# Cached value rows of the samples' attention: pairs in five slots, two of them idle slots of the weight ring

## The chip, the cores and the metric

The kernel runs on one core of one Trainium2 chip. The metric is the device time of one execution in microseconds (us), median of several runs. TensorE is PE, VectorE is DVE, ScalarE is ACT, GpSimd is POOL; SP issues most of the weight DMAs.

## The reference, cut to what matters

The reference is one inference step of a two-layer decoder: a Mamba-2 mixer, then a dilated windowed attention, each followed by a mixture of experts. It runs for one prompt of 256 tokens and for 8 samples of one new token each. The change touches only the samples' attention over their caches, in the second layer:

```
for g, (window, dil) in enumerate(((128, 1), (512, 4), (2048, 16))):
    q, k, v = qkv[:, :, g, 0], qkv[:, :, g, 1], qkv[:, :, g, 2]
    buf = kv_bufs[g]                                  # 8 samples, min(window, 1024) rows, k and v, 16 heads x 64
    k_all = concatenate([buf[:, :, 0], k]); v_all = concatenate([buf[:, :, 1], v])
    idx = wl - dil * arange(window // dil + 1)        # every dil-th row: 128, 128 or 64 of the cache, and the own row
    s = einsum('bshd,bskhd->bshk', q, k_all[:, idx]) * ATTN_SCALE
    p = exp(s - max(s)); l = sum(p)
    outs.append(einsum('bshk,bskhd->bshd', p, v_all[:, idx]) / l)
```

So each sample and each of the three head groups needs 128, 128 or 64 cached value rows of 1024 float32 numbers (512 or 256 KB), 24 such tiles in all. The groups are then combined by their softmax denominators.

## The kernel before, in words

**Engines and order.** Each engine has its own program, written out by hand, and semaphores tie them together. The weights go through a ring of six slots of 2 MB (`ring`), filled by SP in the order of use: ten plus four chunks of the first layer, the 32 experts of layer 0, then 20 chunks of the attention (`ATT_CHUNKS`: 18 of the q, k, v projection and two of the output projection), then the 32 experts of layer 1. A chunk may land when the products that read its slot's last chunk are done.

**The attention.** For each head group g, PE projects 24 column tiles (`qkv_tile`, 16 products of 264 columns each): eight of q, eight of k, eight of v. With the eight v tiles go eight steps t of the prompt's attention: `scores`, the tile, then `lagging(g, t)`, which turns the probabilities of step t - 1 (`turn`, L1200) and multiplies the values of step t - 2 (`values`, L1212). DVE masks and takes maxima (`masked`), divides in the last group (`divided`), and takes the products up (`taken_up`). ACT does the exponents and copies.

**The samples' caches.** POOL loads key rows and queries (`keys`, `query`) into `rows_in`, a tile of `CSLOTS` = 5 slots of 1024 numbers per partition: three slots of keys, two of queries. DVE multiplies and sums them (`cache_scores`; semaphore `k_r`). When all 20 jobs are done, POOL loads the value rows with `cached_values(n)` (L702 to L706) for n = 0 to 23, one tile into slot n % 5 of the same `rows_in`. From the sixth load on it waits for `v_p`, which PE raises once per tile used.

In the last head group, at steps 3 to 6, PE runs `cache_values(i)` (L1266 to L1283), i = 0 to 3, for samples 2i and 2i + 1. It takes the groups in turn; for each it waits for both samples' tiles (`r_l`) and issues eight products at L1279 (the helper splits each float32 product in two). That is six tiles and 24 products for one i: 16 with 128 keys and 8 with 64. The sum for i stands in one bank. DVE masks it (`own_rows(i)`, L2233) one step later, behind `masked` and ahead of `taken_up`, and PE gathers the channels (`own_channels(i)`, L1285, products at L1294) ahead of the next `cache_values`. POOL's stores of the new value rows stand behind all 24 loads in its program.

**The ring's idle slots.** Chunk 14 and chunk 15 of the attention (k tiles 56 to 63 of the last group) lie in slots 4 and 5. In `moe_stream(1)` (L439) SP refills slots 4 and 5 first, on `moes[1].gu` >= 1, then slots 0 and 1 on >= 2, then slots 2 and 3 on the output projection's tiles 3 and 7. Tile 63 raises `moes[1].gu` first and tile 71, the last projected, raises it second; all other tiles raise `q_p`.

Of the kernel before, what the change touches and what calls it, by code (L numbers as in the profile page):

```python
# [12 lines left out]
D = 1024  # L13
DT = D // P
TP = 256
NS = 8
# [28 lines left out]
NGRP = len(PATTERNS)  # L45
KEYS = [min(w, PAST) // dil for w, dil in PATTERNS]
SCALE = HD ** -0.5
NEG = -1.0e30
CSLOTS = 5
KSLOTS = 3  # L50
JOBS = 1 + 2 * DT
CJOBS = [(g, b, 1) for g in range(2) for b in range(NS)] + [(2, b, 2) for b in range(0, NS, 2)]

# [15 lines left out]
RING = 6  # L69
SSM_CHUNKS = (IN_DIM - SH) // 512 + DI * D // (P * CH)  # L70
ATT_CHUNKS = NGRP * 3 * D // 512 + D * D // (P * CH)
STREAM_SLOT = (0, (SSM_CHUNKS + 3 * NE) % RING)
# [3 lines left out]
def bass_hybrid_step(nc, a, outs):  # L76
# [6 lines left out]
    with ExitStack() as ctx:  # L83
# [9 lines left out]
        ring = sb("ring", [P, RING, CH])  # L93
# [55 lines left out]
        m = Area()  # L149
# [40 lines left out]
        m = Area(after_vec)  # L190
        st_in = m(STATES, NS, N)
        outer = m(2, NS, N)
        m = Area(0)
# [4 lines left out]
        m = Area()  # L198
# [25 lines left out]
        m = Area(after_vec + STATES * NS * N)  # L224
# [5 lines left out]
        m = Area(ARENA - DT * (EG + NE))  # L230
# [3 lines left out]
        m = Area()  # L234
# [8 lines left out]
        rows_in = m(CSLOTS, D)  # L243
# [127 lines left out]
        moes = [Moe(0), Moe(1)]  # L371
# [3 lines left out]
        q_p = sem("qkv_projected")  # L375
# [12 lines left out]
        r_l = [sem(f"cache_rows_landed{i}") for i in range(CSLOTS)]  # L388
# [5 lines left out]
        v_p = sem("cache_values_summed")  # L394
# [25 lines left out]
        def cache_rows(g, b, kv):  # L420

            w, dil = PATTERNS[g]
            return caches[g][0, b, :, kv].rearrange("(n s) h d -> s n (h d)", s=dil)[0]

        def wait_chunk(eng, n):

            eng.wait_ge(s_ld[n % RING], 16 * (n // RING + 1))
# [112 lines left out]
        def _(pool):  # L540
# [84 lines left out]
            for t in range(XT_TILES):  # L625
                g = t // TPG
# [53 lines left out]
            def keys(u):  # L680
                g, b, n = CJOBS[u]
                if u >= KSLOTS:
                    pool.wait_ge(k_r, u - KSLOTS + 1)
                for i in range(n):
                    pool.dma_start(rows_in[i * HD:i * HD + KEYS[g], u % KSLOTS, :],
                                   cache_rows(g, b + i, 0)).then_inc(r_l[u % KSLOTS], 16)

            def query(u):
                g, b, n = CJOBS[u]
                slot = KSLOTS + u % 2  # L690
                if u >= 2:
# [7 lines left out]
                    keys(u)  # L699
                    query(u)  # L700

            def cached_values(n):  # L702
                b, g = 2 * (n // 6) + n % 2, n % 6 // 2
                if n >= CSLOTS:
                    pool.wait_ge(v_p, n - CSLOTS + 1)
                pool.dma_start(rows_in[0:KEYS[g], n % CSLOTS, :], cache_rows(g, b, 1)).then_inc(r_l[n % CSLOTS], 16)  # L706

            for g in range(NGRP):
                if g >= 1:
                    cache_jobs(range(NS * (g - 1), NS * g))  # L710
                pool.wait_ge(kv_e, JOBS * g + 1)
                pool.dma_start(q_rows[g].rearrange("b (t d) -> t b d", d=P),
                               q_own).then_inc(q_st, 16)
                if g == NGRP - 1:
                    pool.wait_ge(q_st, 16 * NGRP)
                    cache_jobs(range(2 * NS, len(CJOBS)))
                else:
                    pool.wait_ge(q_st, 16 * (g + 1))
                lo = 1 if g == 0 else 0
                rows = kv_p[g][0, 0].rearrange("(c p) w h d -> p c w (h d)", p=P)  # L720
                own_rows = kv_s[g][0].rearrange("b s w h d -> (s w) b (h d)").rearrange("w b (t d) -> w t b d", d=P)
                for kind in range(2):
                    if g == NGRP - 1 and kind == 1:
                        pool.wait_ge(k_r, len(CJOBS))
                        for n in range(NS * NGRP):
                            cached_values(n)
                    for q in range(2):
                        pool.wait_ge(kv_e, JOBS * g + 1 + DT * kind + 4 * q + 4)
                        pool.dma_start(rows[:, :, kind, 512 * q:512 * q + 512],
                                       KV[:, lo:2, 512 * q:512 * q + 512]).then_inc(kvst, 16)  # L730
                    pool.dma_start(own_rows[kind], kv_own).then_inc(kvst, 16)
# [5 lines left out]
        def _(pe):  # L737
            def transpose(out, in_):
                return pe.transpose(out, in_, ident[0:in_.shape[0], 0:in_.shape[0]])  # L739
# [323 lines left out]
            for i in range(CT):  # L1063
# [5 lines left out]
                for k in range(DT):  # L1069
                    if i == 0:  # L1070
                        tile_ready(0, k)
                    mm = pe.matmul(bank[i % 2][:, 0:T], wv[:, k, (i % 4) * P:(i % 4 + 1) * P], hT[:, k, :],  # L1072
                                   start=(k == 0), stop=(k == DT - 1))
# [23 lines left out]
            for t in range(XT_TILES):  # L1097
                g = t // TPG
# [24 lines left out]
            for d in range(DT):  # L1123
                if d < 2:
                    mm = out_products(d, LAST, XT_TILES)
                else:
# [3 lines left out]
                    mm = out_products(d, 0, XT_TILES)  # L1130
# [14 lines left out]
            def qkv_tile(i):  # L1145

                n = i // 4
                slot = (STREAM_SLOT[1] + n) % RING
                if i % 4 == 0:
                    pe.wait_ge(loads[1][slot], 16 * (n // RING + 1))  # L1150
                if i >= 2:
                    pe.wait_ge(q_e, i - 1)
                wv = ring[:, slot, :].rearrange("p (k n) -> p k n", k=DT)
                for k in range(DT):
                    if i == 0:
                        tile_ready(2, k)
                    mm = pe.matmul(bank[i % 2][:, 0:T], wv[:, k, (i % 4) * P:(i % 4 + 1) * P], hT[:, k, :],  # L1157
                                   start=(k == 0), stop=(k == DT - 1))

                mm.then_inc(moes[1].gu if i in (63, 71) else q_p, 1)  # L1160
                if i == 0:
                    pe.matmul(bank[7][:, 0:P], half[:, :], half[:, :], start=True, stop=True).then_inc(c_p, 1)

            def rows_job(g, j):

                n = JOBS * g + j
                if n:
# [32 lines left out]
            def turn(g, t, h):  # L1200
                n = DT * g + t
                if g < 2:
                    pe.wait_ge(h_e, 4 * (n + 1))
                else:
                    pe.wait_ge(h_n, t + 1)
                if n or h:
                    pe.wait_ge(h_c, 2 * n + h)
                for j in range(3):
                    mm = transpose(bank[4][:, j * P:(j + 1) * P], sm[:, t % 2, h, j * P:(j + 1) * P])
                mm.then_inc(h_t, 1)  # L1210

            def values(g, t):  # L1212
# [50 lines left out]
            before = [sum(j[2] for u, j in enumerate(CJOBS) if u % KSLOTS == slot) for slot in range(KSLOTS)]  # L1263
            before += [sum(j[2] for u, j in enumerate(CJOBS) if u % 2 == slot) for slot in range(2)]

            def cache_values(i):  # L1266
                if i == 0:
                    pe.wait_ge(c_a, 2 * NGRP + 3)
                    pe.wait_ge(c_v, 11)
                else:  # L1270
                    pe.wait_ge(y_o, i)
                for g in range(NGRP):
                    n0, k = 6 * i + 2 * g, KEYS[g]
                    for n in (n0, n0 + 1):
                        pe.wait_ge(r_l[n % CSLOTS], 16 * (before[n % CSLOTS] + n // CSLOTS + 1))
                    for q in range(2):
                        for j in range(2):
                            r = 64 * j + 32 * q
                            mm = pe.matmul(bank[5][r:r + 2 * DT, :], pTs[0:k, g, 2 * i + j:P:NS],  # L1279
                                           rows_in[0:k, (n0 + j) % CSLOTS, 512 * q:512 * q + 512],  # L1280
                                           start=(g == 0), stop=(g == NGRP - 1))
                            if q:
                                mm.then_inc(v_p, 1)  # L1283

            def own_channels(i):  # L1285

# [53 lines left out]
            for d in range(DT):  # L1340
                n = ATT_CHUNKS - 2 + d // 4
                slot = (STREAM_SLOT[1] + n) % RING
# [4 lines left out]
                for k in range(DT):  # L1347
                    if d == 0:
                        pe.wait_ge(h_o, 2 * DT + k + 1)
                    mm = pe.matmul(bank[d % 2][:, 0:T], wv[:, k, (d % 4) * P:(d % 4 + 1) * P], yT[:, k, :],  # L1350
                                   start=(k == 0), stop=(k == DT - 1))
# [10 lines left out]
        def _(act):  # L1362
# [170 lines left out]
            for i in range(CT + 2):  # L1533
                if i < CT:
# [4 lines left out]
                    b = bank[i % 2]  # L1539
# [5 lines left out]
                if i >= 2:  # L1545
                    j = i - 2
# [40 lines left out]
            norm(2, xn_a, gmix(1))  # L1587

            def qkv_done(i):
                if i in (63, 71):  # L1590
                    act.wait_ge(moes[1].gu, 1 if i == 63 else 2)
                else:
                    act.wait_ge(q_p, i + 1 - (i > 63))

            def copy_tile(g, i):

# [110 lines left out]
        def _(v):  # L1707
# [392 lines left out]
            for t in range(XT_TILES + 1):  # L2100
                g = t // TPG
# [129 lines left out]
                v.memset(bank[5][:, :], 0.0).then_inc(c_v, 1)  # L2231

            def own_rows(i):  # L2233
                v.wait_ge(v_p, 6 * i + 6)
                if i >= 1:
                    v.wait_ge(c_p, 4 + i)
                v.tensor_tensor(y_own, bank[5][:, :], own_head, ALU.mult).then_inc(y_o, 1)
                v.wait_ge(c_p, 5 + i)
                v.tensor_copy(y_c[:, 16 * i:16 * i + 16], bank[2][:, 16 * i:16 * i + 16]).then_inc(y_cp, 1)
# [73 lines left out]
```

## Time and profile before

| | us |
|---|---|
| median of 3 runs | 1778.4 |
| lowest, highest | 1776.05, 1779.36 |
| the profiled execution | 1779.78 |
| its span | 1778.1 |
| PE busy | 1667.8 (94%) |
| DVE busy | 642.9 (36%) |
| ACT busy | 451.2 (25%) |
| POOL busy | 132.9 (7%) |
| DMA, mean of the span | 302 GB/s |

Busy shares are averages over stages with different limits. The profile's rows give for each group of instructions how long the engine was busy and how long it stood idle just before, with the name of what ended that wait. "PEclk" is the TensorE clock that was granted, as a share of full speed.

### The profile page before, as it was taken

What the parts mean: (1) busy time and instruction counts of PE and PEld (TensorE: products, weight loads), DVE (VectorE), ACT (ScalarE), POOL (GpSimd) and SP (SyncE); (2) the same over time, 40 slices, a digit from 0 to 9 for tenths busy, and PEclk for the clock granted to TensorE, in tenths of its full rate; (3) what the DMA queues carried; (4) which work ended last, traced back from release to release, by engine and by line L of the source; (5) the groups of instructions that cost most, each with busy time, mean ns of one, the idle gap of its engine ahead of it and who ended that gap; (6) DMA issues with size and microseconds to landing.
All of it is one profiled execution on the core that took longest, in us unless ns stands there. A gap on an engine that the chain in (4) does not pass through costs nothing.

```text
span 1778.1 us, 21545 instructions
## 1 busy us (share of the span) xinstructions
PE 1667.8 (94%) x8029; PEld 971.2 (55%) x8029; DVE 642.9 (36%) x1382; ACT 451.2 (25%) x1166; POOL 132.9 (7%) x280
## 2 busy tenths in 40 slices
PE   7999879899999999999999999887899999999997
PEld 5887666734443344434877778655654443444342
DVE  2558992322222222214034354633432221222123
ACT  3439861211111111112142241222211111111112
POOL 1122430000000000001001002211000000000000
PEclk9999989899999999998999999988999999999999
DMA  9457772389999999999436619935259999999995
GB/s 324 144 169 209 205 241 105 100 339 417 429 429 428 429 428 429 429 428 347 149 108 221 237 64 336 271 118 185 95 227 417 430 429 427 430 429 427 429 428 211
DMA packets 101362, 537.72 MB, mean 302 GB/s; under 512 B 7964, under 2 KB 32740, under 8 KB 76690
## 3 DMA queue, kind: packets, MB, share of 16 engines
q1 hardware_dynamic: 85520, 485.18, 67.3%
q0 software_dynamic: 15360, 51.30, 9.0%
q8 instruction: 40, 0.66, 0.1%
q10 hardware_dynamic: 418, 0.39, 0.1%
q14 instruction: 24, 0.20, 0.0%
HBM read 520.61 MB, written 16.42 MB: 302 GB/s over the span
## 4 chain that ended last, share of the span: by engine, by line
PE 65%; DMA 17%; DVE 11%; ACT 3%; issue 2%; POOL 0%; SPq 0%; ACTq 0%; DVEq 0%
PE bank L834 20%; DMA ring<-in_moe_w_gate_up 13%; PE bank L1157 9%; PE bank L846 8%; PE bank L820 6%; PE bank L1072 5%; PE bank L739 4%; PE bank L1115 3%; PE bank L840 3%; DMA arena<-sample_queries 2%; PE bank L1350 2%; DVE arena L2072 2%; ACT arena L1654 1%; PE bank L1195 1%; DVE arena L2080 1%
## 5 line engine op out<-in xcount | busy, mean ns | idle before, releaser
L834 PE MATMUL bank<-ring,arena 128*64 128x512 f32 x2048 | 448.1, 593 | 20.6 <-DMA ring<-in_moe_w_gate_up 19.4
L834 PEld LDWEIGHTS bank<-ring,arena 128*64 128x64 f32 x2048 | 153.9, 137 | 308.2 <-issue 308.2
L1157 PE MATMUL bank<-hT,ring 128*128 128x264 f32 x1152 | 274.2, 395 | 0.0
L1157 PEld LDWEIGHTS bank<-hT,ring 128*128 128x128 f32 x1152 | 218.8, 194 | 46.0 <-issue 10.1
L846 PE MATMUL bank<-ring,arena 128*64 128x512 f32 x1024 | 226.8, 595 | 0.0
L1933 DVE TENSOR_TENSOR arena<-arena,bank 128x512 f32<-128x512 f32 x32 | 34.3, 1071 | 412.8 <-ACT arena L1436 412.8
L846 PEld LDWEIGHTS bank<-ring,arena 128*64 128x64 f32 x1024 | 70.6, 137 | 134.9 <-issue 134.9
L840 PE MATMUL bank<-arena 128*128 128x512 f32 x272 | 134.9, 618 | 1.7 <-ACT arena L1446 1.6
L739 PE MATMUL bank<-ident,arena 128*128 128x128 f32 (+6 forms) x609 | 104.9, 286 | 30.0 <-DMA arena<-in_ssm_d 10.4
L739 PEld LDWEIGHTS bank<-ident,arena 128*128 128x128 f32 (+6 forms) x609 | 73.6, 146 | 92.6 <-issue 46.5
L1436 ACT ACTIVATE arena<-bank 128x512 f32<-128x512 f32 x32 | 19.1, 597 | 412.7 <-PE bank L834 412.7
L1881 DVE SCALAR_TENSOR_TENSOR arena<-arena 128x1024 f32<-128x1024 f32 x34 | 43.7, 1284 | 211.4 <-ACT arena L1446 211.2
L820 PE MATMUL bank<-arena 128*128 128x224 f32 x512 | 103.8, 363 | 0.0
L1876 DVE TENSOR_TENSOR X<-X,bank 128x512 f32<-128x512 f32 x136 | 90.2, 683 | 26.8 <-PE bank L840 26.8
L820 PEld LDWEIGHTS bank<-arena 128*128 128x128 f32 x512 | 99.1, 197 | 0.8
L1072 PE MATMUL bank<-hT,ring 128*128 128x264 f32 x384 | 92.1, 401 | 0.0
L840 PEld LDWEIGHTS bank<-arena 128*128 128x128 f32 x272 | 45.9, 188 | 69.4 <-issue 51.4
L1072 PEld LDWEIGHTS bank<-hT,ring 128*128 128x128 f32 x384 | 75.1, 198 | 13.7 <-issue 0.4
L1613 ACT ACTIVATE arena<-bank 128x264 f32<-128x264 f32 x72 | 27.6, 384 | 156.5 <-PE bank L1157 156.5
L1444 ACT ACTIVATE arena<-bank 128x512 f32<-128x512 f32 x32 | 19.1, 597 | 189.5 <-PE bank L846 189.5
L1115 PE MATMUL bank<-arena,ring 128*128 128x264 f32 x256 | 62.5, 404 | 0.0
L1866 DVE TENSOR_TENSOR arena<-bank,vcol 128x448 f32<-128x448 f32 x64 | 40.0, 624 | 59.3 <-PE bank L820 59.3
(322 smaller groups left out, 1550.2 us busy)
## 6 DMA issues: line engine op xcount, KB each, us to landing
ring<-in_moe_w_gate_up SPq DMA_DIRECT2D x128, 2048.0 KB, 16.3
ring<-in_moe_w_down SPq DMA_DIRECT2D x64, 2048.0 KB, 12.9
ring<-in_attn_qkv SPq DMA_DIRECT2D x18, 2048.0 KB, 8.9
ring<-in_ssm_in_proj SPq DMA_DIRECT2D x10, 2048.0 KB, 15.3
arena<-in_cache_kv_w POOLq DMA_DIRECT2D x32, 512.0 KB, 6.9
out<-arena POOLq DMA_DIRECT2D x24, 512.0 KB, 3.9
ring<-in_ssm_out_proj SPq DMA_DIRECT2D x4, 2048.0 KB, 10.2
arena<-in_state_ssm SPq DMA_DIRECT2D x16, 512.0 KB, 4.8
```

Of the source, the lines that this page charges most:

```text
L739: return pe.transpose(out, in_, ident[0:in_.shape[0], 0:in_.shape[0]])
L820: mm = pe.matmul(bank[4 + i % 2][:, c * 4 * FREE:(c + 1) * 4 * FREE], xn_e[:, t, d * P:(d + 1) * P], Pm[:, t, :, :].rearrange("p e s -> p ...
L834: mm = pe.matmul(bank[j][e * SLOTS:(e + 1) * SLOTS, :], Xg[:, 4 * half + k, 2 * h + e, :], weights(2 * half + e)[:, k, j * DE:(j + 1) * DE ...
L840: pe.matmul(bank[6 + j % 2][:, :], CmT[:, (j // 2) * P:(j // 2 + 1) * P], ysl[:, j % 2, :], start=True, stop=True).then_inc(s.sc, 1)
L846: mm = pe.matmul(bank[2 + q][e * SLOTS:(e + 1) * SLOTS, :], actT[:, k, e * SLOTS:(e + 1) * SLOTS], weights(4 + e)[:, k, q * 512:(q + 1) * ...
L1072: mm = pe.matmul(bank[i % 2][:, 0:T], wv[:, k, (i % 4) * P:(i % 4 + 1) * P], hT[:, k, :], start=(k == 0), stop=(k == DT - 1))
L1115: mm = pe.matmul(bank[d % 2][:, 0:T], wv[:, k, (d % 2) * P:(d % 2 + 1) * P], conv_out[:, k, :], start=(k == 0), stop=(k == XT_TILES - 1))
L1157: mm = pe.matmul(bank[i % 2][:, 0:T], wv[:, k, (i % 4) * P:(i % 4 + 1) * P], hT[:, k, :], start=(k == 0), stop=(k == DT - 1))
L1350: mm = pe.matmul(bank[d % 2][:, 0:T], wv[:, k, (d % 4) * P:(d % 4 + 1) * P], yT[:, k, :], start=(k == 0), stop=(k == DT - 1))
L1866: v.tensor_tensor(Xg[:, 2 * i:2 * i + 2, :, NS:SLOTS], bank[4 + i % 2][:, 0:8 * FREE].rearrange("p (d e s) -> p d e s", d=2, e=4), gffn_fo ...
L1876: v.tensor_tensor(xs, xs, bank[6 + j % 2][:, :], ALU.add).then_inc(done, 1)
L1881: v.scalar_tensor_tensor(out=acc_s[:, :, :], in0=ysl[:, :, :], scalar=wcol[:, bass.ds(n, 1)], in1=acc_s[:, :, :], op0=ALU.mult, op1=ALU.ad ...
```

## The change

The value rows land in pairs, one pair for both samples of a step and one group, in five pair slots (`VSLOTS`). Pair slots 0 to 3 are halves of ring slots 4 and 5, and pair slot 4 is the first two slots of `rows_in`. Each pair is still loaded with two DMAs. Up to ten loads are out at once. `v_p` is raised once per pair, and a load of pair m from 5 on waits for `v_p` >= m - 4. Ahead of the first load POOL waits for all 64 tiles up to tile 63 (`q_p` >= 64), after which nobody reads the ring's slots 4 and 5. Tile 63 therefore raises `q_p` like the others; tile 71 raises `moes[1].gu` first, and the first transpose of the last prompt step raises it second. So SP refills ring slots 4 and 5 after tile 71 and slots 0 and 1 after that transpose.

```diff
+VSLOTS = 5
+        def value_rows(m):
+            if m % VSLOTS == VSLOTS - 1:
+                return rows_in[:, 0:2, :]
+            slot = (STREAM_SLOT[1] + ATT_CHUNKS - 6 + m % VSLOTS // 2) % RING
+            at = m % VSLOTS % 2 * 2 * D
+            return ring[:, slot, at:at + 2 * D].rearrange("p (j d) -> p j d", j=2)
...
-            def cached_values(n):
-                b, g = 2 * (n // 6) + n % 2, n % 6 // 2
-                if n >= CSLOTS:
-                    pool.wait_ge(v_p, n - CSLOTS + 1)
-                pool.dma_start(rows_in[0:KEYS[g], n % CSLOTS, :], cache_rows(g, b, 1)).then_inc(r_l[n % CSLOTS], 16)
+            def cached_values(m):
+                i, g = m // NGRP, m % NGRP
+                if m >= VSLOTS:
+                    pool.wait_ge(v_p, m - VSLOTS + 1)
+                for j in range(2):
+                    pool.dma_start(value_rows(m)[0:KEYS[g], j, :],
+                                   cache_rows(g, 2 * i + j, 1)).then_inc(r_l[m % VSLOTS], 16)
...
                         pool.wait_ge(k_r, len(CJOBS))
-                        for n in range(NS * NGRP):
-                            cached_values(n)
+                        pool.wait_ge(q_p, 64)
+                        for m in range(NS // 2 * NGRP):
+                            cached_values(m)
...
-                mm.then_inc(moes[1].gu if i in (63, 71) else q_p, 1)
+                mm.then_inc(moes[1].gu if i == 71 else q_p, 1)
...
                     mm = transpose(bank[4][:, j * P:(j + 1) * P], sm[:, t % 2, h, j * P:(j + 1) * P])
+                    if n == NGRP * DT - 1 and h == 0 and j == 0:
+                        mm.then_inc(moes[1].gu, 1)
...
-                    n0, k = 6 * i + 2 * g, KEYS[g]
-                    for n in (n0, n0 + 1):
-                        pe.wait_ge(r_l[n % CSLOTS], 16 * (before[n % CSLOTS] + n // CSLOTS + 1))
+                    m, k = NGRP * i + g, KEYS[g]
+                    slot = m % VSLOTS
+                    pe.wait_ge(r_l[slot], 16 * before[slot] + 32 * (m // VSLOTS + 1))
...
-                                           rows_in[0:k, (n0 + j) % CSLOTS, 512 * q:512 * q + 512],
+                                           value_rows(m)[0:k, j, 512 * q:512 * q + 512],
                                            start=(g == 0), stop=(g == NGRP - 1))
-                            if q:
-                                mm.then_inc(v_p, 1)
+                    mm.then_inc(v_p, 1)
...
             def qkv_done(i):
-                if i in (63, 71):
-                    act.wait_ge(moes[1].gu, 1 if i == 63 else 2)
+                if i == 71:
+                    act.wait_ge(moes[1].gu, 1)
                 else:
-                    act.wait_ge(q_p, i + 1 - (i > 63))
+                    act.wait_ge(q_p, i + 1)
...
             def own_rows(i):
-                v.wait_ge(v_p, 6 * i + 6)
+                v.wait_ge(v_p, NGRP * i + NGRP)
```

## Rows read from the trace of the kernel before

**Rows 1.** The page: the chain that ended last, by engine, shares of the span.

```profile
PE 65%; DMA 17%; DVE 11%; ACT 3%; issue 2%; POOL 0%; SPq 0%; ACTq 0%; DVEq 0%
```

**Rows 2.** Waits, 1130 to 1300 us: total us, times, longest us.

```profile
POOL arena L706 <- PE bank L1279: 60.6, 7, 20.3
...
PE bank L1279 <- DMA arena<-in_cache_kv_w: 12.3, 4, 3.2
```

**Rows 3.** PE in order of time: start us, us, what, [idle before <-releaser].

```profile
1156.23 0.66 PE L1221 MATMUL bank<-ident,arena 128*64 128x128 f32 x8
1156.71 0.82 PE L1227 MATMUL bank<-arena 128*64 128x256 f32 x8
1157.46 0.55 PE L739 MATMUL bank<-ident,arena 128*128 128x128 f32 x3
...
1164.88 1.92 PE L1279 MATMUL bank<-arena 128*16 128x512 f32 x16 [1.09 <-issue]
1169.94 1.91 PE L1279 MATMUL bank<-arena 64*16 64x512 f32 x8 [3.14 <-DMA arena<-in_cache_kv_w]
...
1181.74 1.93 PE L1279 MATMUL bank<-arena 128*16 128x512 f32 x16
...
1207.51 0.55 PE L739 MATMUL bank<-ident,arena 128*128 128x128 f32 x3
...
1213.69 1.06 PE L1294 MATMUL bank<-quarter,arena 128*128 128x4 f32 x8 [0.47 <-DVE arena L2237]
1214.67 1.93 PE L1279 MATMUL bank<-arena 128*16 128x512 f32 x16
1219.47 1.06 PE L1279 MATMUL bank<-arena 64*16 64x512 f32 x8 [2.87 <-DMA arena<-in_cache_kv_w]
1220.46 0.66 PE L1221 MATMUL bank<-ident,arena 128*64 128x128 f32 x8
...
1229.65 0.66 PE L1221 MATMUL bank<-ident,arena 128*64 128x128 f32 x8
```

**Rows 4.** L706's time to landing, and POOL in order of time.

```profile
DMA to landing us min/median/max: 3.3/5.8/9.5
...
1143.26 2.67 POOL L706 DMA_DIRECT2D arena<-in_cache_kv_w  x5
1166.24 2.17 POOL L706 DMA_DIRECT2D arena<-in_cache_kv_w  x4 [20.32 <-PE bank L1279]
```

**Rows 5.** Stretches: length, busy us of each engine, granted clock, DMA share, GB/s.

```profile
1050.00:1067.00 17.00, 15.79 (x119) 12.07 (x118) 8.34 (x27) 9.22 (x39) 0.00 (x0) 1.00 0.07 14
1143.00:1155.00 12.00, 7.90 (x43) 5.99 (x42) 7.92 (x28) 5.03 (x22) 2.92 (x6) 0.72 0.80 245
1229.00:1241.00 12.00, 9.30 (x71) 6.42 (x70) 4.93 (x18) 3.83 (x13) 1.34 (x2) 0.74 0.96 365
1400.00:1500.00 100.00, 98.40 (x438) 42.54 (x440) 25.26 (x42) 14.35 (x24) 0.00 (x0) 1.00 1.01 429
```

**Rows 6.** DVE in order of time, in the third step of the values.

```profile
1207.63 0.42 DVE L2193 TENSOR_TENSOR arena<-arena,bank 128x256 f32<-128x256 f32 x1 [8.66 <-PE bank L1227]
...
1212.94 0.69 DVE L2237 TENSOR_TENSOR arena<-bank,arena 128x512 f32<-128x512 f32 x1
```

**Rows 7.** SP's issues in order of time, and two pieces of the chain.

```profile
1130.19 99.03 SPq L455 DMA_DIRECT2D ring<-in_moe_w_gate_up  x4
...
1300.44 0.64 DVE arena L1866
...
1301.11 13.97 PE bank L834 x64
```

**Rows 8.** PE in order of time, two projected tiles of the second head group.

```profile
1021.73 0.52 PE L739 MATMUL bank<-ident,arena 128*128 128x128 f32 x3 [1.64 <-ACT arena L1662]
...
1023.03 5.52 PE L1157 MATMUL bank<-hT,ring 128*128 128x264 f32 x16
...
1031.59 3.83 PE L1157 MATMUL bank<-hT,ring 128*128 128x264 f32 x16
```

## The prediction

> **What bounds the kernel now.** I read from coarse to fine. The chain that ended last gives 65% of the span to TensorE (PE), 17% to DMAs, 11% to DVE [rows 1], so an edit pays where PE waits on that chain. The changed loads feed one stretch, the samples' cached values, so I took the waits of 1130 to 1300 us: PE at L1279 stood 12.3 us in 4 waits for cache rows (up to 3.2 us each), and POOL at L706 stood 60.6 us in 7 waits for L1279 [rows 2]. These are the two sides of one ring. A step i of the values takes six tiles, two of each group; the ring has five slots; so the step's sixth tile is issued only after the step's first products have released a slot. The page shows it: POOL issues five loads from 1143.26 us, then nothing until 1166.24 us, when PE has done its first eight products [rows 4]. PE's order of time shows the other side: 16 products at 1164.88, none until 1169.94 us, 3.14 us idle and put down to the cache load [rows 3]. The same hole follows in each of the next three steps, from 1181.74 us on; the last measures 2.87 us [rows 3].
>
> The hole costs more than its length. Behind it the same work runs slower: the eight products of the 64 keys take 1.91 us at 1169.94 us and 1.06 at 1219.47 us [rows 3]. The step from 1164.88 to 1181.74 us is 16.86 us long; only 3.14 of that is the hole [rows 3].
>
> Further down, the attention's end and the router lead to the experts, whose first product at 1301.11 us follows DVE, not a DMA [rows 7]. From there on the 16 DMA engines are busy throughout, 1.01 of 1.00 at 429 GB/s [rows 5]: that stage is set by its weight stream, which is refilled as PE uses the ring up. It begins when PE reaches it, so time saved ahead of it moves the whole stage forward.
>
> **The change, part by part.**
>
> (a) Five pair slots for five tile slots. Each load remains one tile, 24 in all, but now ten are on their way at once. The first five pairs m = 0 to 4 go out without a wait; pair 5, the third of the second step, waits for the first pair's products. That is 1166 us, and it is wanted some 12 us later, at 1164.88 + 11.3 + 1.9 us (below). A load takes 3.3 to 9.5 us to land [rows 4], so it is there. Pairs 6 and 7 go out with the second and third third of step 0 and are wanted two steps on; pairs 8 to 11 likewise have a step or more. All four holes go: 12.3 us.
>
> (b) The slow work behind the holes. I rebuild a step from pieces at the full clock: 16 products 1.9 us (1.92 at 1164.88), the last eight 1.0 (1219.47 to 1220.46), L1221 0.5 and L1227 0.75 (starts 1156.23, 1156.71, 1157.46), and the rest from transposes through scores, tile and own channels 7.15 us (1207.51 to 1214.67) [rows 3]. Sum 11.3 us. Four of them are 45.2 us; the four steps of before run from 1164.88 to 1229.65 us, 64.8 us [rows 3]. **Gain 19.6 us**: 12.3 of holes, the rest clock, less what comes next.
>
> (c) What is late next. The 7.15 us piece already holds it: PE stood 0.47 us for DVE at 1213.69 us [rows 3]. DVE starts at 1207.63 us, once the head's values are done, and ends own_rows at 1212.94 + 0.69 us [rows 6], 6.0 us later, while PE's own work to that point is 5.6 us. At the full clock all four steps meet this, where before only one did. So 0.5 us per step is given back, and it is inside the 11.3.
>
> (d) Doubled pile at the start. POOL issues ten loads, 0.53 us each (2.67 us for five [rows 4]), done at 1148.6 us. Step 0 wants three pairs (2.5 MB), and all ten are 4.5 MB. From 1143 to 1155 us the DMAs moved 245 GB/s while 0.80 busy [rows 5], which is 306 GB/s when busy: three pairs by about 1152 us, all ten by 1158 to 1162 us, before PE arrives at 1164.88 us even if they land mixed. Cost 0; without that cover each us past 1164.88 would be a us of PE.
>
> (e) POOL's new wait for the 64th projected tile. Queued behind it are the value loads and then the stores of the new rows. SP issues the experts' first chunk on that very tile at 1130.19 us [rows 7], 13 us before POOL gets there. Cost 0. The stores of the second kind come after the loads as before, and earlier by the clock; only POOL's end waits for them.
>
> (f) The experts' first four gate-up chunks. Before, two go out at 1130.19 us and two after the last projected tile, 99.03 us from the first [rows 7]. Now two wait for that last tile and two for the transpose that follows; SP has nothing else queued behind them before the down chunks, which wait for the output projection anyway. With the shift that is about 1209 us and a few us later, for use at 1301.11 less 19.6, 1281.5 us. Their 8.4 MB at the 365 GB/s of 1229 to 1241 us, where two of the chunks landed [rows 5], is 23 us: there by about 1237 us, 44 us of cover. Cost 0. Their absence from 1130 to 1141 us leaves the last query and key loads more room, between 0 and 0.5 us; I take 0.
>
> (g) Half as many increments of the products' semaphore, one increment moved to another tile, another base address of the moving operand: the same instructions on every engine, 0.
>
> The sum against the profiled execution, 1779.8 us: 1760.2. The median of the runs is 1778.4 us, 1.4 lower, and the same sum against it gives **1758.8 us**.
>
> **The rivals.**
>
> R1, **slower: PE never comes back to its full clock between the tiles.** The granted clock has two levels, 2.4 and 1.2 GHz (1.00 and 0.50 of full). Most of a step here isn't dense product: transposes, 4-column and 16-wide products, and a 0.5 us wait. An idle of 1.64 us followed by light work was enough to make the tile at 1023.03 us take 5.52 us where the next one took 3.83 [rows 8]. If whole steps ran at 1.2 GHz, PE's 10.8 us of work would take 10.8 x 1.91/1.06 = 19.4 us, four steps 77.8 us, 13 us more than now: 1791 us. It decides from 19.6/(19.4 - 11.3) = 2.4 slow steps out of four. Against it: 1050 to 1067 us, prompt steps with as many transposes and PE idle for 1.2 of 17 us, ran at 1.00 [rows 5], and the piece from 1207.51 with its 0.47 us wait was followed by products at full speed [rows 3]. Chance 0.04. The Trainium skill ("TensorE: Matmul & The Clock Gate", Part 4: PE-mode transpose) has a rule on this side: transposes don't engage the full clock. By it steps so rich in transposes would tend to R1's time; the trace disagrees, with 1.00 over a stretch as rich in them [rows 5], and I go by the trace.
>
> R2, **some steps lose the clock, or pairs land late.** A drop as in the first step of before costs 16.86 - 3.14 - 11.3 = 2.4 us; holes gone but all four drops kept give 1778.4 - 12.3 = 1766.1 us. Late pairs cost the same order: pair 5 landing after 15 us instead of 9.5 is 3 us of PE. Together 1761.5 to 1768. For it: the tile behind the 1.64 us idle at 1021.73 us was slow; the work behind the 0.47 us at 1213.69 us was not [rows 3, 8]; and no row of before shows four such steps in a row without holes. Chance 0.20.
>
> R3, **it doesn't do what it says**: the loads hold each other up and the wait only moves to the first pair. Past 1164.88 us they reach only if the 4.5 MB run below 4.5 MB/21.6 us = 208 GB/s, against 245 with gaps [rows 5]; and to use up the 19.6 us they would need 4.5 MB/41 us = 110 GB/s. Then the time is 1775 to 1779. Chance 0.03.
>
> R4, **the early chunks were needed.** To use up the gain they would have to land after 1301 us, 8.4 MB in 92 us or 91 GB/s; the nearest row has 365 [rows 5]. Under 0.01, counted with R1.
>
> R5, **more than forecast**: DVE's 0.5 us doesn't come in every step and the query loads shorten: up to 2.0 + 0.5 us more, and with the runs' own spread 1754 to 1757. Chance 0.08.
>
> **How the numbers follow.** The forecast, 1757 to 1761.5, has 0.65. The measurement can tell about 0.2%, 3.6 us, from no change. The forecast with R2's lower three quarters (0.14) and most of R5 makes the range 1755 to 1766, slightly over 0.8. Faster: forecast, R2 and R5, 0.93. Within 0.2%: R3, 0.03. Slower: R1 and R4, 0.04.
>
> **What would show it.** Waits of L1279 for cache rows gone, or under 0.5 us; POOL's loads in one group of ten at about 1143 us; steps of 11.3 us between the starts of the 16 products, with about 0.5 us before each own_channels put down to DVE; clock near 1.00 from 1164 to 1210 us; the chain's first expert product near 1281.5 us and released by DVE; four gate-up chunks issued close together near 1209 us; the experts' stage as long as before. The prediction is wrong if the clock shows drops without holes (R1, R2), if a wait for cache rows stands at the first product (R3), or if the first expert product waits for its ring (R4).

## The result, and the profile after

The changed kernel takes 1756.8 us, median of 4 runs (1755.7 to 1757.7), against 1778.9 us before (1776.1 to 1780.9; four runs, of which the table above has three). The ratio is 0.9876, 95% interval 0.9856 to 0.9896: 22.1 us less, between 18.5 and 25.6. The forecast was 1758.8 us, in a range of 1755 to 1766. The profiled execution has a span of 1756.0 us, 22.1 less than before's.

In the waits of 1130 to 1300 us the row PE L1279 <- cache rows of before [rows 2] has no successor (the line is L1294 now). POOL still waits for products, but for 34.2 us instead of 60.6, and nobody waits for it. Total us, times, longest us:

```profile
POOL ring L717 <- PE bank L1294: 34.2, 3, 18.0
...
PE bank L752 <- ACT arena L1676: 4.1, 1, 4.1
...
```

PE in order of time (start us, us, what, [idle before <-releaser]) is the view that answers to [rows 3]:

```profile
1162.05 2.92 PE L1294 MATMUL bank<-ring,arena 128*16 128x512 f32 x24 [1.09 <-issue]
1164.90 0.66 PE L1236 MATMUL bank<-ident,arena 128*64 128x128 f32 x8
...
1167.47 3.83 PE L1170 MATMUL bank<-hT,ring 128*128 128x264 f32 x16
...
1172.31 1.05 PE L1308 MATMUL bank<-quarter,arena 128*128 128x4 f32 x8 [0.46 <-DVE arena L2251]
1173.29 1.07 PE L1294 MATMUL bank<-ring,arena 128*16 128x512 f32 x8
...
1184.54 2.92 PE L1294 MATMUL bank<-ring,arena 128*16 128x512 f32 x24
...
1195.79 1.07 PE L1294 MATMUL bank<-arena 128*16 128x512 f32 x8
...
1207.04 0.66 PE L1236 MATMUL bank<-ident,arena 128*64 128x128 f32 x8
```

All 24 products of a step now run without a hole, in 2.9 us. The steps start at 1162.05, 1173.29, 1184.54 and 1195.79 us and the last ends at 1207.04: 11.25 us each, 45.0 in all, where before took 64.8. Of the waits inside the steps only DVE's 0.46 to 0.48 us ahead of each L1308 is left.

POOL in order of time answers to [rows 4]: ten loads at once, then six behind the products of step 0, then six and two.

```profile
1140.17 4.26 POOL L717 DMA_DIRECT2D ring<-in_cache_kv_w  x8
1144.42 1.05 POOL L717 DMA_DIRECT2D arena<-in_cache_kv_w  x2
1163.44 3.16 POOL L717 DMA_DIRECT2D ring<-in_cache_kv_w  x6 [17.97 <-PE bank L1294]
1174.70 1.04 POOL L717 DMA_DIRECT2D ring<-in_cache_kv_w  x2 [8.10 <-PE bank L1294]
1175.73 1.08 POOL L717 DMA_DIRECT2D arena<-in_cache_kv_w  x2
1176.80 1.04 POOL L717 DMA_DIRECT2D ring<-in_cache_kv_w  x2
1185.93 1.04 POOL L717 DMA_DIRECT2D ring<-in_cache_kv_w  x2 [8.09 <-PE bank L1294]
```

The stretches (length, busy us of PE, PEld, DVE, ACT and POOL, granted clock, DMA share, GB/s) answer to [rows 5]. The clock is 1.00 through the four steps. The pile of loads keeps the DMAs busy until about 1159 us, 3 us before the first of them is wanted.

```profile
1143.00:1155.00 12.00, 10.13 (x54) 7.62 (x54) 5.78 (x20) 6.37 (x28) 2.47 (x5) 0.72 0.99 280
1155.00:1162.00 7.00, 5.96 (x37) 4.81 (x35) 5.66 (x18) 2.30 (x10) 0.00 (x0) 1.00 0.38 153
1162.00:1174.00 12.00, 11.49 (x88) 7.23 (x92) 5.83 (x18) 3.93 (x19) 3.16 (x6) 1.00 0.71 216
1174.00:1185.00 11.00, 10.52 (x81) 6.74 (x77) 5.84 (x18) 3.19 (x14) 3.15 (x6) 1.00 0.80 238
```

SP's order of time answers to [rows 7]: the four gate-up chunks leave at 1205.07 us and over the next 7 us, 73 us ahead of their first use. The chain's first expert product stands at 1277.66 us, behind DVE as before.

```profile
1205.07 7.04 SPq L464 DMA_DIRECT2D ring<-in_moe_w_gate_up  x4
1235.19 21.02 SPq L464 DMA_DIRECT2D ring<-in_moe_w_down  x2
```

**Where the 22.1 us of the two profiled executions lie.** SP issues the third and fourth weight chunk of the first layer's experts (the mark, below) at 299.69 us before and at 297.04 us after: 2.65 us have nothing to do with the change, which begins some 800 us later. From there to the first cached value product it is 865.2 and 865.0 us. The four steps take 19.8 us less. The two heads behind them, up to the output projection, take 10.5 us instead of 11.5. The rest up to the first expert product is equal within 0.2 us, and the experts' stage takes 478.3 us instead of 477.0.

### The profile page after: what moved, and what is told of

Its sections match the earlier page's. It is cut to its first block, busy times and chain, and to the rows that moved or that the text cites. A ratio compares the mean times of both kernels' runs of the same rounds, so it can differ in the third digit from the quotient of the medians.

```text
span 1756.0 us, 21537 instructions
## 1 busy us (share of the span) xinstructions
PE 1657.3 (94%) x8029; PEld 964.8 (55%) x8029; DVE 642.8 (37%) x1382; ACT 451.8 (26%) x1166; POOL 133.3 (8%) x280
## 4 chain that ended last, share of the span: by engine, by line
PE 65%; DMA 17%; DVE 11%; ACT 4%; issue 2%; POOL 0%; SPq 0%; ACTq 0%; DVEq 0%
PE bank L847 21%; DMA ring<-in_moe_w_gate_up 13%; PE bank L1170 8%; PE bank L859 8%; PE bank L833 6%; PE bank L1085 5%; PE bank L752 4%; PE bank L853 4%; PE bank L1128 3%; DMA arena<-sample_queries 2%; PE bank L1364 2%; ACT arena L1668 1%; DVE arena L2086 1%; DVE arena L2168 1%; PE bank L1208 1%
```

## The experiments

The theory: the gain is the four holes, 12.3 us, and the half-speed work behind them, some 7 us; nothing else in the change has a price. The rivals: the clock's part isn't the hole's doing; the depth matters beyond the six tiles of a step; the moved expert chunks carry part of the time.

**The changed kernel again, twice** (no edit).

> The changed kernel once more, beside the others of this call. The theory (four holes of 12.3 us and the half-speed work behind them of 7.3 us are what went) expects 1757 +- 1.5 us, steps of 11.25 us between the starts of the cached value products, and puts the 2.8 us by which the first such product came earlier in the first profile down to the spread between executions: here it may stand anywhere within 3 us of 1164.9 us. The rival (the early start is the change's own, by freeing the DMAs from the experts' two chunks at 1130 us) expects it at 1162 us again, with the difference to before arising after 1130 us.

Measured: 1755.3 us (ratio 0.9884, 0.9863 to 0.9905), 0.2 below the band I had given. Steps of 11.25 us again (1160.48, 1171.72, 1182.97, 1194.22 us) and no wait for cache rows. The first product stood at 1160.48 us, 4.4 us ahead of 1164.9 where I had allowed 3, so by the position alone the rival would stand. But the mark stood at 295.91, so 864.6 us lie between, against 865.2 before. The early start is the spread of the first 300 us, not the change's: over all traces the mark lies between 294.65 and 300.24 us, at 295.28 in the kernel before with eight filler products and at 300.24 in the changed kernel with four slots. The second time:

> The changed kernel beside the other three, for comparison: 1755 to 1757 us, steps of 11.25 us, no wait for cache rows, 115.6 us from the first cached value product to the first expert product.

Measured: 1756.2 us (0.9882, 0.9864 to 0.9901), steps of 11.25 us, 115.4 us from the first cached value product to the first expert product.

**The expert chunks' move alone**, on the kernel before:

```diff
-                mm.then_inc(moes[1].gu if i in (63, 71) else q_p, 1)
+                mm.then_inc(moes[1].gu if i == 71 else q_p, 1)
...
+                    if n == NGRP * DT - 1 and h == 0 and j == 0:
+                        mm.then_inc(moes[1].gu, 1)
```

> The kernel before with one part of the change alone: the experts' first two chunks start after the last projected tile instead of 11 tiles earlier, the next two at the following transpose. The theory (44 us of cover) expects the time of before, 1778.9 +- 1.5 us, and the four holes as they were. The rival (these chunks slowed the last query and value loads at 1130 us) expects 2 to 3 us less, 1776 us; a second rival (they are late for the first expert product) expects more.

Measured: 1777.1 us, ratio 0.9997 (0.9985 to 1.0008): no difference. The holes stayed, 12.5 us in 4 waits, and the first cached value product came 865.0 us after the mark, as before. So neither is the move late, nor did the early chunks slow the query and value loads by anything that shows. Its trace shows the clock's part once more. A step with a hole of 3.30 us took 15.64 us here (1181.20 to 1196.84), the one after it with 3.06 us 16.49:

```profile
1181.20 1.92 PE L1281 MATMUL bank<-arena 128*16 128x512 f32 x16
1186.42 1.07 PE L1281 MATMUL bank<-arena 64*16 64x512 f32 x8 [3.30 <-DMA arena<-in_cache_kv_w]
...
1196.84 1.92 PE L1281 MATMUL bank<-arena 128*16 128x512 f32 x16
1201.82 1.91 PE L1281 MATMUL bank<-arena 64*16 64x512 f32 x8 [3.06 <-DMA arena<-in_cache_kv_w]
```

**The hole filled with useless products**, on the kernel before. This takes the idle away and leaves the loads and their wait:

```diff
+                    if g == NGRP - 1:
+                        for _ in range(FILL):
+                            pe.matmul(bank[3][:, 0:3 * P], ident[:, :], mask[:, 0, :], start=True, stop=True)
```

First with FILL = 8:

> The kernel before with eight more 384-column products on PE ahead of each wait for the 64-key tiles, whose result nobody reads: they fill the hole without touching the loads, 2.9 us of the 3.1. The theory (the hole itself costs 12.3 us, and the half speed behind it another 7.3) expects the step to keep the hole's length but to run on at full clock: steps of 14.4 us instead of 16.2 on average, 7.1 us less in all, 1771.8 us. The rival (PE runs slow there for another reason, light work for one) expects half clock behind the filled hole as before and no change, 1778.9 us.

Measured: 1778.2 us, ratio 1.0004 (0.9991 to 1.0016). By the time alone the rival would have won. The trace says otherwise: I had the filler's size wrong by nearly two. It takes 5.36 us, not 2.9, so the steps are 11.25 + 5.36 = 16.6 us, and the filler pushed out what the clock gave back. The clock was 1.00 in all four steps, where before had 0.80, 0.80, 0.89 and 0.89.

```profile
1163.02 1.93 PE L1283 MATMUL bank<-arena 128*16 128x512 f32 x16 [1.09 <-issue]
1164.87 5.43 PE L1277 MATMUL bank<-arena,ident 128*128 128x384 f32 x16
1170.23 1.06 PE L1283 MATMUL bank<-arena 64*16 64x512 f32 x8
...
1179.62 1.93 PE L1283 MATMUL bank<-arena 128*16 128x512 f32 x16
```

Then with FILL = 4:

> The filler again, half as long: four 384-column products ahead of each wait for the 64-key tiles. Eight of them took 5.36 us, 2.2 us more than the hole, so that trial made the steps 16.6 us long at a granted clock of 1.00 and moved no time. Four take 2.7 us and leave 0.4 us of the hole. The theory (the hole costs 12.3 us and the half speed behind it another 7) expects steps of 14.4 us, the granted clock at 1.00 and 7 us less than before, 1770.5 us. The rival (what the clock gives back is taken by DVE or another wait at once) expects steps over 15.5 us and under 3 us of gain.

Measured: 1770.2 us, ratio 0.9950 (0.9934 to 0.9967), 8.1 us less. The filler takes 2.8 us and PE still waits up to 0.62 us for the load; the four steps take 57.7 us:

```profile
1162.74 1.92 PE L1283 MATMUL bank<-arena 128*16 128x512 f32 x16 [1.09 <-issue]
1164.60 2.85 PE L1277 MATMUL bank<-arena,ident 128*128 128x384 f32 x8
1167.73 1.07 PE L1283 MATMUL bank<-arena 64*16 64x512 f32 x8 [0.28 <-DMA arena<-in_cache_kv_w]
...
1177.12 1.93 PE L1283 MATMUL bank<-arena 128*16 128x512 f32 x16
...
1182.45 1.06 PE L1283 MATMUL bank<-arena 64*16 64x512 f32 x8 [0.62 <-DMA arena<-in_cache_kv_w]
```

```profile
1164.00:1181.00 17.00, 16.25 (x102) 9.59 (x95) 5.83 (x18) 3.43 (x14) 5.29 (x10) 1.00 0.57 175
1181.00:1198.00 17.00, 15.44 (x100) 8.71 (x98) 5.83 (x18) 3.43 (x14) 3.15 (x6) 1.00 0.60 188
```

This splits the gain. 64.8 to 57.7 is the clock, 7.1 us; 57.7 to 45.0 is the hole, 12.7 us. The clock stayed at 1.00 in all four steps here, and in the changed kernel without any filler, with the same light work in both. So the idle of some 3 us is what took the clock away, not the light work around it.

**The depth.** The change with three, two and four pair slots (six, four and eight tiles on their way); the edit is one number:

```diff
-VSLOTS = 5
+VSLOTS = 3
```

> Three pair slots instead of five, so six tiles on their way instead of ten. The theory: what counts is that a whole step's six tiles fit, so that no step waits for its own products; pair 3 goes out when pair 0 is used, about 10 us before it is wanted, and 2.5 MB need 8 to 9 us; 0 to 1.5 us of waits in all, 1757 to 1759 us. The rival (the deeper pile is needed, since three pairs land in 9 us plus up to 3 us) expects a wait of 2 to 3 us in each of the last three steps and the clock lost behind it, 1765 to 1771 us.

Measured with three: 1760.1 us, 0.9904 (0.9884 to 0.9924), 4.8 us over the changed kernel measured beside it (1755.3). I expected at most 1.5 us of waits and 1759 us; there are 3.9 us of them, three holes in two of the steps, which take 14.0 and 12.7 us, the other two 11.25. The rival's mechanism is there, at half its size, and the clock isn't lost behind it: 1.00 from 1162 to 1211 us. The four steps take 49.3 us instead of 45.0.

```profile
1173.26 1.07 PE L1294 MATMUL bank<-ring,arena 128*16 128x512 f32 x8
1175.18 1.07 PE L1294 MATMUL bank<-ring,arena 128*16 128x512 f32 x8 [0.85 <-DMA ring<-in_cache_kv_w]
1177.91 1.06 PE L1294 MATMUL bank<-arena 64*16 64x512 f32 x8 [1.67 <-DMA arena<-in_cache_kv_w]
...
1201.90 1.06 PE L1294 MATMUL bank<-arena 64*16 64x512 f32 x8 [1.42 <-DMA arena<-in_cache_kv_w]
```

Six loads leave together behind a step's products, and the last is up to 11.7 us on its way; a step lasts 11.25. So a ring that holds exactly one step's tiles has no slack.

> Two pair slots, four tiles on their way, otherwise the change as it is (base addresses, pairs, half the increments, the later expert chunks). The theory (the third pair of a step can go out only when the first is used) expects the four holes back, 3.4 to 3.8 us each, with the clock lost behind them: 1777 to 1781 us. The rival (pairs or addresses bring part of the gain by themselves) expects under 1772 us.

Measured with two: 1779.7 us, 1.0016 (1.0005 to 1.0027). The holes are back and longer, 17.4 us in 4 waits (4.4 us each, where I expected 3.4 to 3.8), the steps take 68.7 us together. Pairs, addresses and half the increments bring nothing by themselves.

> Four pair slots, eight tiles on their way. With three the pile that goes out during step 0 was up to 11.7 us on its way and PE waited 0.85, 1.67 and 1.42 us. With four, pair 4 is the first that waits for a product; it and pair 5 are wanted a third of a step later than pairs 3 and 4, which are already there. The theory (slack of a third of a step is worth 1 to 2 us per wait) expects 0 to 1 us of waits in all and the time of five slots, within 1 us. The rival (only ten in flight cover the pile) expects 2 us or more of waits and 2 to 4 us more than with five.

Measured with four: 1756.6 us, 0.9878 (0.9859 to 0.9896), no wait for cache rows, steps of 11.25 us, 115.3 us from the first cached value product to the first expert product. The same as five. The rival fell: eight in flight are enough, six are not.

**The experts' chunks held back** to the last tile of the output projection, in the changed kernel:

```diff
                         sp.wait_ge(s.gu, pair * 2 + (j // 2 + 1))
+                        if l == 1 and isinstance(pair, int):
+                            sp.wait_ge(s.dn, 2)
```

> The changed kernel, with the experts' first four chunks held back until the last tile of the output projection (some 50 us later than in the changed kernel). The theory: they are wanted only from the first expert product on, and the experts' stage is set by a weight stream that otherwise stands still until 1285 us; 8.4 MB from about 1256 us are there by 1276 us, and the down chunks by 1286 us; 0 to 2 us more, 1757 to 1759 us. The rival (the stream never catches up a late start) expects the delay of the first refill to show in full, 5 us or more.

Measured: 1759.1 us, 0.9895 (0.9879 to 0.9911), some 3 us over the changed kernel's runs (1755.3 to 1756.8), though the intervals overlap. The six chunks leave between 1257.88 and 1261 us and the first refill at 1286.43 us, when the DMAs are still at the end of that pile (1.00 busy from 1279 to 1289 us, 0.32 in the changed kernel). The first expert product comes as early as ever (115.2 us after the first cached value product); the experts' stage takes 479.9 us instead of the 477.0 to 478.3 of the kernel before and the changed one. I had the last chunk landed by 1286 us. By this one trace a delay of 50 us costs 2 to 3; the change's own delay is inside the cover.

**The reordering**, a version that could beat both. DVE masks the samples' rows ahead of the prompt's masks, and PE takes `cache_values` ahead of `own_channels`:

```diff
-                        if s >= 4:
-                            own_channels(s - 4)
                         cache_values(s - 3)
+                        if s >= 4:
+                            own_channels(s - 4)
```

> A version that could beat both: DVE masks the sample rows ahead of the prompt's masks, and PE takes the next cached values ahead of gathering the channels, so that the 2.85 us of value products cover what PE waited for DVE. The theory (0.47 us of DVE in each of the four steps is all that is left late there) expects steps of 10.8 us and 1755 us. The rival (DVE's chain through masks, exponents and divisions takes its place) expects steps of 11.25 us again and no change from 1757 us, or up to 1 us more.

Measured: 1755.2 us, 0.9870 (0.9848 to 0.9892), level with the changed kernel's 1755.3. The steps are 10.7 us (10.8 expected) and DVE's waits in them gone, 2.4 us over the four. The two heads behind them give nearly all of it back, 12.6 us instead of 10.5. In the last prompt step DVE's masks come later, ACT's exponents and copies with them, and PE waits 1.23 us for a copy (L1676) that it didn't wait for before. But its wait for DVE's last division (L2191) falls from 2.12 to 0.67 us, so the two waits together are no longer than the one was. What grew is the work at half speed: the granted clock is 0.51 from 1206.2 to 1216.3 us, against 0.74 from 1210.9 to 1217.5 us in the changed kernel. The second version keeps DVE's old order in the last step and puts the last `own_channels` behind the head's values:

```diff
-                    elif s == 7:
-                        own_channels(3)
                 if 2 <= s <= DT + 1:
                     values(g, s - 2)
+                if g == NGRP - 1 and s == 7:
+                    own_channels(3)
```

> The reordering again, with the last step as in the changed kernel for DVE's masks, and own channels behind the head's values on PE there. The first reordering took 2.35 us from the four steps and gave 1.8 us of it back in the two heads that follow, where PE waited for ACT's copy of the probabilities (1.2 us) that stood behind DVE's later masks. The theory expects both gone: first expert product 2 to 3 us earlier after the first cached value product than in the changed kernel (115.6 us there), 1753 us. The rival (the last two heads are bound by their own chain of division, transpose and product) expects 114.5 us or more again and no change in the time.

Measured: 1753.0 us, 0.9869 (0.9847 to 0.9890), 3.2 us under the changed kernel measured beside it (1756.2). The intervals of the two overlap, so the time alone doesn't prove it; the traces carry it: 112.2 us from the first cached value product to the first expert product (1160.01 to 1272.18), 115.4 to 115.6 in the changed kernel.

```profile
1203.09 1.05 PE L1308 MATMUL bank<-quarter,arena 128*128 128x4 f32 x8
1204.58 0.52 PE L752 MATMUL bank<-ident,arena 128*128 128x128 f32 x3 [0.44 <-ACT arena L1676]
1206.03 1.33 PE L752 MATMUL bank<-ident,arena 128*128 128x128 f32 x5 [0.93 <-DVE arena L2191]
```

PE's wait for DVE's last division (L2191) falls from 2.12 to 0.93 us, with 0.44 us for ACT's copy. The two waits are 0.5 us shorter than in the first version, which is a small part of what this one gains on it. Most of that is clock again, 0.78 from 1204.6 to 1212.5 us, and why the drop is shorter here isn't shown. Against the changed kernel it gains what the four steps save and 0.75 us of waits.

## Why the prediction was right, point by point

(a) Right: 12.3 us of holes gone. Its bound was too kind, though. I took the landing time from loads that travel five or fewer at a time, 9.5 us at most; with ten it rises to 14.2 us. Five slots hide that. With three, where six travel together and take up to 11.7 us, the same reasoning would have failed, as that run showed.

(b) Right and the core of it: steps rebuilt from pieces at the full clock gave 11.3 us, measured 11.25; four of them 45.2, measured 45.0. The filled hole shows the split, 12.7 us of hole and 7.1 of clock, where the sum had 12.3 and 7.3.

(c) Right: 0.46 to 0.48 us for DVE in each of the four steps, where before had one.

(d) Right: the ten loads done at about 1159 us, no wait at the first product. (e) Right: nothing waits for POOL. (f) Right: the chunks leave 4 us earlier than I had them, the move alone measures 0.9997, and holding them back another 50 us costs 2 to 3 us. The 0 to 0.5 us that I left open for the query loads is 0: 865 us from the mark to the first product with and without the early chunks.

The sum was 19.6 us and the medians moved by 22.1, within the interval of 18.5 to 25.6. By the two profiled executions the steps gave 19.8 us. Of the other 2.3, some 1.3 are the first 300 us of the kernel (2.65 us less) and the experts' stage (1.3 us more), and both differ as much between executions of one kernel: the mark stood between 294.65 and 300.24 us, and the experts' stage took 477.0 to 478.3 us. These parts are chance, and so is how close the median came to the forecast within them.

The remaining 1.0 us is in the two heads behind the steps, and the sum had no term for it. It isn't the holes' clock loss reaching into them. In the kernel before PE was back at full speed ahead of the heads (its last projected tile, at 1224.56 us, takes 3.83 us, as all of the changed kernel's). In both kernels PE then waits 2.12 us for DVE and works at half speed for a while behind it, and how long that lasts differs. The eight products of L1227 before, L1242 after, take 0.82 us at full speed. In the second head they took 1.49 us before (first lines) and 0.82 after (second):

```profile
1233.56 0.77 PE L739 MATMUL bank<-ident,arena 128*128 128x128 f32 x5 [2.12 <-DVE arena L2177]
...
1238.87 1.49 PE L1227 MATMUL bank<-arena 128*64 128x256 f32 x8
```

```profile
1210.94 0.76 PE L752 MATMUL bank<-ident,arena 128*128 128x128 f32 x5 [2.12 <-DVE arena L2191]
...
1216.24 0.82 PE L1242 MATMUL bank<-arena 128*64 128x256 f32 x8
```

The heads took 10.5 to 10.6 us in all five traces with four or five slots and 11.4 to 11.5 us in the kernel before and with the chunks' move alone. But they took 11.3 us with the hole filled by four products, where no step lost the clock, and 10.6 us with two slots, where all steps had a hole. So neither the holes nor the steps' clock decides it, and the cause stays open.

**The rivals.** R1 and the clock's part of R2 fell: the clock was 1.00 in all steps, with the light work, the transposes and a 0.47 us wait in each. The Trainium skill ("TensorE: Matmul & The Clock Gate", Part 4: PE-mode transpose) says that transposes don't engage the full clock. This trace doesn't bear it out for transposes mixed with products: 1.00 from 1162 to 1185 us. R2's other part, late pairs, is real but needs a smaller ring: 4 to 5 us with three slots. R3 fell: no wait stands at the first product, and the pile moved at 280 GB/s. Two slots come to R3's time, but by another way, the hole at each step's third pair as in the kernel before. R4 didn't happen, and a delay of 50 us, once tried, cost 2 to 3 us. R5's band, 1754 to 1757, holds the measured time, but not by its reasons: DVE's wait came in every step, and the query loads gave nothing.

## What to carry to other kernels

A ring must hold what one step uses and enough beyond that to cover the time that its loads take when they travel together. Here six tiles are one step's and still cost waits, eight don't. Price a hole on PE by the length of the step with and without it, built from pieces at full clock, not by the hole alone: here 12.3 us of idle were 19.8 us of time. And check where a buffer is idle before asking for memory; two slots of the weight ring were free here for 78 us (from the 64th tile at about 1127 us to the refill at 1205.07), and their next load had cover to spare.

## What the runs showed of the hardware that I had not expected

Holes of nearly one length cost the clock differently: after 3.30 us the next products ran at full speed and the step lost 1.1 us beyond the hole, after 3.06 us they ran at half speed at once and it lost 2.2 (15.64 and 16.49 us less the hole, against 11.25). Holes of 0.85, 1.67 and 1.42 us in the run with three slots lost nothing, while one of 1.64 us had slowed a tile in the kernel before [rows 8]. The wait of 2.12 us ahead of the heads was followed by half-speed work in ten of the eleven traces that have it (granted clock 0.74 from 1210.9 to 1217.5 us in the changed kernel, heads of 10.5 us), but not with three slots (1.00 from 1211 to 1220 us, heads of 8.9). So the length of one idle doesn't tell its price here.

Loads of 512 KB that travel in tens take up to 14.2 us to land instead of 9.5, at 280 GB/s with the DMAs 0.99 busy, against 429 GB/s for the weights' chunks. More of them in flight raised the busy share, but not the mean rate while busy (306 GB/s before, 283 now). The rate isn't even: within this one pile it was 195 GB/s from 1151 to 1153 us and 408 from 1155 to 1157, the DMAs 0.99 busy or more in both. The value rows come in pieces of 4 KB throughout, so that alone doesn't explain it, and no run tested what does.
